# Hybrid decoder step: weight sums with two rooms and a step of lag, raw blocks loaded from ScalarE's queue, phase turn and gate-weight loads rearranged

## What is computed

```
h  = rms_norm(x) * (1 + scale(c)) + shift(c)
layer 0: q,k,v,z,gate = h @ w_in_ab       # GLA and RetNet, chunked linear attention
         y = (norm(attention) * silu(z)) @ w_out_ab
layer 1: qkv, z, b, a = h @ w_in_c        # gated DeltaNet; qkv through a causal convolution of width 4
         y = (norm(delta) * silu(z)) @ w_out_c
x  = x + gate(c) * rms_norm(y)
```

## Time and profile before

| | |
|---|---|
| median of 3 runs | 2617.94 us (2615.05 to 2620.39) |
| the profiled execution, its own time | 2615.59 us |
| its span in the profile | 2613.8 us |
| TensorE busy | 2371.3 us (91%) |
| VectorE, ScalarE, GpSimd busy | 1416.1, 968.0, 872.4 us |
| mean granted clock of TensorE, of full speed | 0.957 |
| phases by the first and last TensorE instruction | inab to 722, mixab 728 to 1118, inc 1125 to 1782, mixc from 1793 us |

### The profile page before, as it was taken

How to read it: one execution, slowest core, us unless ns; L and a number is a source line. 1 busy time by engine, 2 the same in 40 slices (tenths; PEclk the granted TensorE clock), 3 DMA queues, 4 the chain that set the end, 5 groups by cost and what they waited for, 6 DMA issues and landing times. The chain is left out here.

```text
span 2613.8 us, 58705 instructions
## 1 busy us (share of the span) xinstructions
PE 2371.3 (91%) x23067; PEld 1693.5 (65%) x23084; DVE 1416.1 (54%) x3034; ACT 968.0 (37%) x2726; POOL 872.4 (33%) x1092
## 2 busy tenths in 40 slices
PE   6989679679979999769999999996999999999997
PEld 2434234234555655258888888785888888888885
DVE  3332544534057785547777585555646555564655
ACT  3533244233311111324444343433444454444431
POOL 2541122121111111112322122115655656565652
PEclk9999899889989999879999999998999999999997
DMA  8543575572346444586676667556523222222213
GB/s 296 149 143 102 154 213 144 165 217 77 113 133 234 154 160 148 167 276 213 213 213 215 198 198 228 179 165 184 133 65 94 79 83 91 83 91 75 82 38 85
DMA packets 371527, 395.26 MB, mean 151 GB/s; under 512 B 39215, under 2 KB 262511, under 8 KB 371298
## 3 DMA queue, kind: packets, MB, share of 16 engines
q1 hardware_dynamic: 337186, 360.28, 43.8%
q10 hardware_dynamic: 34112, 31.71, 4.0%
HBM read 275.19 MB, written 116.72 MB: 150 GB/s over the span
## 5 line engine op out<-in xcount | busy, mean ns | idle before, releaser
L2728 DVE SCALAR_TENSOR_TENSOR inc_acc<-inc_ub,inc_taps,inc_acc 128x512 f32<-128x512 f32 x288 | 243.7, 846 | 9.2 <-ACT inc_acc L2571 2.4
L742 PE MATMUL inab_b<-inab_wt,keep 128*128 128x512 f16 x768 | 172.6, 387 | 30.9 <-ACT inab_vz L1064 20.0
L742 PE MATMUL inab_b<-inab_wt,raw_next 128*128 128x512 f16 x768 | 173.8, 390 | 21.1 <-ACT inab_vz L1064 21.1
L2507 POOL COPY inc_halo<-inc_ub 128x3 f32<-128x3 f32 x96 | 50.2, 525 | 363.6 <-DVE inc_ub L2716 224.1
L1344 PE MATMUL mixab_y<-keep,mixab_oT_hi 128*128 128x512 f16 x512 | 152.4, 379 | 7.1 <-DVE mixab_f_y L1424 5.4
L742 PEld LDWEIGHTS inab_b<-inab_wt,keep 128*128 128x128 bf16 (+1 forms) x768 | 75.9, 99 | 125.7 <-ACT inab_vz L1064 22.2
L742 PEld LDWEIGHTS inab_b<-inab_wt,raw_next 128*128 128x128 bf16 (+1 forms) x768 | 76.5, 100 | 117.3 <-ACT inab_vz L1064 23.3
L726 POOL TENSOR_TENSOR inab_a_out<-inab_stage,inab_a_out 128x384 f16<-128x384 f32 x64 | 61.3, 958 | 226.9 <-ACT inab_a_out L719 226.9
L712 DVE TENSOR_TENSOR inab_stage<-inab_m,inab_stage 128x512 f16<-128x512 f32 x64 | 44.1, 689 | 135.9 <-ACT inab_stage L722 135.9
L2837 PE MATMUL inc_b<-inc_room,keep 128*128 128x256 bf16 (+3 forms) x864 | 109.9, 279 | 2.4 <-DVE stage_next L2698 2.4
L3201 POOL TENSOR_TENSOR mixc_levels<-mixc_BT,raw_next 128x512 f32<-128x512 f32 (+1 forms) x82 | 110.3, 1376 | 1.5 <-DVE mixc_BT L3487 1.5
(11 more groups left out here) (619 smaller groups left out, 6363.4 us busy)
## 6 DMA issues: line engine op xcount, KB each, us to landing
keep<-tmp_w SPq DMA_DIRECT2D x336, 256.0 KB, 3.2
tmp_qkv<-inc_acc SPq DMA_DIRECT2D x96, 256.0 KB, 2.6
inab_stage<-in_w_in_c SPq DMA_DIRECT2D x128, 128.0 KB, 2.5
...
tmp_w<-inab_a_out SPq DMA_DIRECT2D x64, 192.0 KB, 2.1
...
```

The source lines that it names most:

```text
L742: last = nc.tensor.matmul(dst, lhs(a, k), rhs(b, k), start=(k == 0 and i == 0), stop=(k == KT - 1 and i == len(PASSES) - 1))
L2507: pool.tensor_copy(halo[:, g, :], ub[w % 2][side][:, BLK:]).then_inc(halo_saved[side], 1)
L2728: ins = dve.scalar_tensor_tensor(a_v, u_[:, i:i + BLK], taps[:, g, i:i + 1], a_v, ALU.mult, ALU.add)
```

## The change

- **The pair weights.** `a_out` gets two rooms. On ScalarE the high halves of the sums of step n are made in step n + 1 (`sums_hi`), on VectorE the low halves of the sums two steps later, and SyncE's store of them is issued two steps later. The raw quarters of step n + 1 are loaded from ScalarE's queue in step n, no longer from SyncE's.
- **Which groups.** No step lies at g = 10, 15 and 16 any more, and three groups instead of seven have two. Blocks 1 and 2 have 25 steps each, block 3 has 14. The eight steps of the output weights move to g = 23 to 30 of block 3.
- **SyncE's order.** The store of `r` and the loads of x tiles move to later places among the stores of v and z, and the waits for `u` and `r` to have landed move to g = 24. Two small tables are loaded late, into the room of `a_out`.
- **The turn.** `scale_high` and the copy of `eye2` come before the last state update, GpSimd's part of the halves is dropped; VectorE makes three of the seven low parts, partly between the last steps of mixab, and the four that are left at the start of inc (`first_left`). The second ring slot is loaded at the start of inc instead of the end of mixab.
- **inc.** The z weights are loaded in eight smaller transfers at units 1, 2, 5 and 8. `ORDER` has five qkv units first, and the last two units of a block are z. The last tail rows and sample convolution move to unit 15 of the last block, before the last unit's final products.

```diff
+        if n >= 2:
+            self.store_s(sp, n - 2)
         sp.wait_ge(self.a_lo, n + 1)
-        sp.dma_start(self.dst[u, 0:3, :, k].rearrange("m p e x -> p m e x"), self.a_out[:]).then_inc(self.a_stored, 16)
-        if n + 2 < PAIR_STEPS:
-            sp.wait_ge(self.s_done, n + 1)
-            self.load(sp, n + 2)
-        if n >= 1:
-            self.store_s(sp, n - 1)
+        sp.dma_start(self.dst[u, 0:3, :, k].rearrange("m p e x -> p m e x"), self.a_out[n % 2]).then_inc(self.a_stored[n % 2], 16)
...
+        if n >= 2:
+            self.sums_lo(dve, n - 2)
         dve.wait_ge(self.raw_in[n % 2], 32 * (n // 2 + 1))
-        wait(dve, self.s_hi, n - 1)
         wait(dve, self.s_lo, n - 1)
...
     def hi(self, act, n):
 
+        if n >= 1:
+            self.sums_hi(act, n - 1)
+            if n + 1 < PAIR_STEPS:
+                act.wait_ge(self.a_lo, n)
+                self.load(act, n + 1)
         act.wait_ge(self.raw_in[n % 2], 32 * (n // 2 + 1))
-        wait(act, self.a_stored, 16 * n)
-        act.activation(self.a_out[:, :, 0, :], self.raw[n % 2][:, P:4 * P].rearrange("p (m x) -> p m x", m=3), ACT.Copy).then_inc(self.a_hi, 1)
+        wait(act, self.a_stored[n % 2], 16 * (n // 2))
+        act.activation(self.a_out[n % 2][:, :, 0, :], self.raw[n % 2][:, P:4 * P].rearrange("p (m x) -> p m x", m=3), ACT.Copy).then_inc(self.a_hi, 1)
+
+    def sums_hi(self, act, n):
         act.wait_ge(self.s_done, n + 1)
         wait(act, self.s_stored[n % 2], 16 * (n // 2))
         act.activation(self.s_out[n % 2][:, :, 0, :], self.banks[n % 2][:].rearrange("p (m x) -> p m x", m=4), ACT.Copy).then_inc(self.s_hi, 1)
...
-    W7_TWICE = (16, 18, 20, 22, 24, 26, 28)
-    w7_slots = [g for g in order(BLK) for _ in range(2 if g in W7_TWICE else 1) if not 5 <= g < 7]
-    W7_BLOCK = len(w7_slots)
+    W7_SLOTS = (0, 1, 2, 3, 4, 7, 8, 9, *range(17, 31))
+    W7_TWICE = (20, 24, 28)
+    w7_slots = [g for g in W7_SLOTS for _ in range(2 if g in W7_TWICE else 1)]
...
     def w7_at(b, g):
 
-        return [(b - 1) * W7_BLOCK + i for i, s in enumerate(w7_slots) if s == g] if 1 <= b <= 2 else []
-
-    assert 2 * W7_BLOCK == PAIR_STEPS
+        if b == nb - 1:
+            first = (nb - 2) * W7_BLOCK
+            return [first + i for i, s in enumerate(W7_SLOTS) if s == g and s < W7_LAST]
+        return [(b - 1) * W7_BLOCK + i for i, s in enumerate(w7_slots) if s == g] if 1 <= b < nb else []
+
+    ROWS_AT = {W7_LAST + i: i for i in range(KT)}
+    assert (nb - 2) * W7_BLOCK + sum(s < W7_LAST for s in W7_SLOTS) == PAIR_STEPS
...
+            w7_next(b, 0, 1)
+            next_x(0)
+            w7_next(b, 2, 3, 4, 7, 8)
+            next_x(1)
+            w7_next(b, 9)
+            store_u()
...
                 w7_next(b, 15 + j)
-                if j == 4:
...
+                if j == 1:
+                    next_x(2)
+                if j == 3:
+                    store_r()
+                if j == 6:
                     next_x(3)
+                if j == 9:
+                    sp.wait_ge(out, 80 * (b + 1))
+                    sp.sem_inc(u_free, 1)
+                    sp.sem_inc(r_free, 1)
...
+                  [stage_next[:, i * D:(i + 1) * D].rearrange("p (k n) -> p k n", k=4) for i in (2, 3, 0, 1)])
+    io["first_left"] = early.left()
...
-        for u in range(2):
-            for m in FIRST_NEEDED:
-                sp.dma_start(ring_slot(io, u)[:, m].rearrange("p k e x -> p (k e x)"), io["w7"][u, m].rearrange("p k e x -> p (k e x)")
-                             ).then_inc(io["ring_in"][u][m], 16)
+        first_weights(sp, io, 0)
...
-        early.lower_rest(pool)
...
+        early.upper_sums(act, (0, 1, 2))
         fin.square_sample(act, nt)
+        early.upper_sums(act, (3,))
...
         for p in range(PAIRS):
+            if p == PAIRS - 1:
+                early.scale_high(dve)
+                dve.tensor_copy(eye2.rearrange("p (e c) -> p e c", e=2), bc(tv["eye_h"].unsqueeze(1), [P, 2, HB])).then_inc(eye_ready, 1)
...
-        early.scale_high(dve)
         dve.wait_ge(cond.mm, 6)
...
-        early.lower(dve)
-        dve.wait_ge(o_done, nt + 1)
-        dve.tensor_copy(eye2.rearrange("p (e c) -> p e c", e=2), bc(tv["eye_h"].unsqueeze(1), [P, 2, HB])).then_inc(eye_ready, 1)
+        early.lower_first(dve)
         fin.mean_sample(dve, nt)
+        early.lower(dve, 2)
         dve.wait_ge(gate_in, 48)
         fin.gated_sample(dve, nt, 0, 16 * (nt // 2 + 2))
+        early.lower(dve, 1)
...
-    ORDER = (0, 1, 2, (0, 0), 3, 4, 5, (0, 1), 6, 7, 8, (1, 0), 9, 10, 11, (1, 1))
+    ORDER = (0, 1, 2, 3, 4, (0, 0), 5, 6, (0, 1), 7, 8, 9, 10, 11, (1, 0), (1, 1))
...
+        tiles.load(sp, 0)
+        sp.dma_start(wab_raw, io["w_in_c"].rearrange("(k p) n -> p k n", p=P)[:, :, N_C - 32:N_C]).then_inc(wab_in, 16)
+        first_weights(sp, io, 1)
+        tiles.load(sp, 1)
         load_tables(sp, tab_in, tab, names, io["table"])
...
-        for v in range(4):
-            sp.dma_start(zw[:, v].rearrange("p m k e x -> p m (k e x)"), io["w7"][QKV + v].rearrange("m p k e x -> p m (k e x)")
-                         ).then_inc(zw_in[v // 2], 16)
-        sp.dma_start(alog[:, 0, :], io["a_log_c"].unsqueeze(0).to_broadcast([P, H])).then_inc(small_in, 16)
-        sp.dma_start(alog[:, 1, :], io["dt_bias_c"].unsqueeze(0).to_broadcast([P, H])).then_inc(small_in, 16)
...
+        def load_zw(v):
+            for ms in (slice(0, 4), slice(4, 7)):
+                sp.dma_start(zw[:, v, ms].rearrange("p m k e x -> p m (k e x)"), io["w7"][QKV + v, ms].rearrange("m p k e x -> p m (k e x)")
+                             ).then_inc(zw_in[v // 2], 16)
+
+        ZW_AT = {1: 0, 2: 1, 5: 2, 8: 3}
...
+                if n in ZW_AT:
+                    load_zw(ZW_AT[n])
...
+                if p == 15:
+                    sample_silu(2)
+                    take_tails(2)
...
+        for dst, src, hi in io["first_left"]:
+            dve.tensor_tensor(dst, src, hi, ALU.subtract).then_inc(first_lo, 1)
...
+                if p == 15:
+                    sample_conv(2)
...
+            if n == 0 and i in FIRST_LEFT:
+                pe.wait_ge(first_lo, FIRST_LEFT[i])
```

More of the change, by code:

```diff
@@ L661, in __init__ @@
         self.src, self.dst, self.raw, self.s_out, self.banks = src, dst, raw, s_out, banks
-        self.a_out = ph.sb("a_out", [P, 3, 2, P], F16)
+        self.room = ph.sb("a_out", [P, 6 * P])
+        self.a_out = [self.room[:, i * 3 * P:(i + 1) * 3 * P].bitcast(F16).rearrange("p (m e x) -> p m e x", m=3, e=2) for i in range(2)]
         s = ph.sem
@@ L968, in _ @@
         sp.wait_ge(pre_in, 64)
-        sp.wait_ge(w7.a_stored, 16 * PAIR_STEPS)
-        for i in range(2):
-            sp.wait_ge(w7.s_stored[i], 16 * PAIR_STEPS // 2)
+        w7.stored(sp, w7.s_stored)
         for i in range(4):
@@ L1006, in _ @@
                     w7.lo(pool, step)
-        prep.rstd(pool, nt, 0, NS)
-        prep.split_lo(pool, nt, 0, NS, prep.at(nb))
-        for u in range(KT):
-            rows_out.lo(pool, u)
+        for g in order(BLK):
+            if g == SQUARE[0]:
+                prep.rstd(pool, nt, 0, NS)
+            if g == HI_S:
+                prep.split_lo(pool, nt, 0, NS, prep.at(nb))
+            for step in w7_at(nb - 1, g):
+                w7.lo(pool, step)
+            if g in ROWS_AT:
+                rows_out.lo(pool, ROWS_AT[g])
     @block.scalar
@@ L1099, in groups @@
                 if g in rows_at:
+                    if g == W7_LAST:
+                        w7.sums_hi(act, PAIR_STEPS - 1)
+                        w7.raw_free(act)
+                        rows_out.load(act, 0)
+                        w7.stored(act, w7.s_stored)
                     rows_out.hi(act, rows_at[g])
@@ L1108, in _ @@
             groups(b, BLK, [(4 * b + 4 + tc, P) for tc in range(4)])
-        w7.room_free(act)
-        rows_out.load(act, 0)
-        groups(nb - 1, BLK, [(nt, NS)], rows_at={**dict(zip(range(16, 30, 2), range(7))), 30: 7})
+        groups(nb - 1, BLK, [(nt, NS)], rows_at=ROWS_AT)
         groups(nb, NS, [])
@@ L1139, in w7_sums @@
                 for step in w7_at(b, g):
[L1140 to L1141 removed]
                     w7.sums(dve, step)
+                if b == nb - 1 and g == W7_LAST:
+                    w7.sums_lo(dve, PAIR_STEPS - 2)
+                    w7.sums_lo(dve, PAIR_STEPS - 1)
         def work(b, n, next_tiles):
```

129 lines of the change are left out of this document (69 added, 60 removed).

## The result

The changed kernel takes 2475.49 us in the median of four runs (2470.28 to 2478.14), beside 2616.49 of the kernel before, measured along with it. The ratio is 0.9458, with a 95% interval of 0.9435 to 0.9482.

What follows compares the result with a forecast made beforehand. TensorE was taken to set the pace, with idle and low-clock time to give back. From 2615.59 us, -96 - 10 - 8.5 + 1.5 - 3 = -116 gave 2499.6, stated as 2501 allowing for scatter; range 2488 to 2530.

Steps and rivals of the forecast that it cites:

- read the stretches from block start to block start: First reading step, on inab: blocks 1 and 2 take 177.73 and 181.83 us, block 3 134.66; 38 and 42 us idle.
- Blocks 1 to 3: -96: inab, pair weights: blocks fall to 132, 132 and 130 us, together -96 us (bounds -84 and -106).
- 4 us that I leave for waits that this reading misses: Blocks 1 to 3 of inab: 4 us taken off the 100.3 us gain, leaving -96.
- The second room takes the 4.1 us loop off ScalarE: Pair weights in inab: ScalarE's step becomes about 3.6 us with waits, against 5.22 us of a TensorE group.
- the groups 10, 15 and 16, during which VectorE rotates `r`, carry no step: inab: with SyncE's later wait for `r`, said to change the row of ScalarE's 18.04 us wait; no separate size.
- Rival B: inab blocks: half of the block stalls stay, gain 50 instead of 96 us, about 2547 us; chance 0.14.
- D: inab blocks: ScalarE, with the issues on its queue, becomes the bound and the kernel is slower, 2664 us; chance 0.03.
- The turn: -10: Between mixab and inc: difference no longer stretched, reduction not waiting for the copy; -10 us (bounds -6 and -12).
- inc: -7: inc: start -8.5 us from spreading the z transfers (bounds -9.5 and +8), body +1.5 us.
- The +1.5 for `sample_conv`: Body of inc: of its 4.7 us of VectorE work in the last unit, 1.4 don't fit; +1.5 us (0 to 4).
- Rival C: Units 1 to 3 of inc: z transfers delay ring refills, the 8.5 us return as a wait, 2517 us; chance 0.10.
- The end: -3: Step from inc to mixc: only the last unit's own eviction and store are left; -3 us (0 to -5).

Runs made afterwards that it cites:

- r_first: Changed kernel, but SyncE stores r and waits for u and r to have landed ahead of a block's first store of v; 2496.8 us, ratio 0.954.
- before_r_late: Kernel before, but SyncE stores r behind the fourth store of v, x tiles 2 and 3 load later, u and r waits at g = 24; 2585.6 us.
- spread: Changed kernel with 25, 25 and 14 steps but none doubled, so g = 10, 15 and 16 carry a step each in blocks 1 and 2; 2473.8 us.
- old_groups: Changed kernel with the steps at the groups of before: 32 each in blocks 1 and 2, seven groups doubled, none in block 3; 2519.4 us.
- only_groups: Changed kernel with one room for a_out, no lag of the sums, and r stored and landed ahead of the first v store; 2512.0 us.
- avoid: Changed kernel with 32, 32 and 0 steps in blocks 1 to 3, g = 10, 15 and 16 free, ten groups doubled; 2518.8 us.
- gpsimd_low: Changed kernel, but GpSimd makes one of the seven low parts at the end of mixab, beside VectorE's differences; 2480.3 us, ratio 0.948.

## Why the prediction was wrong, point by point

**Block 0 isn't in the sum: 11.1 us.** The step that failed is the first one, "read the stretches from block start to block start", in which I took blocks 1 to 3 for all that could give something back. The order of SyncE's stores is the same in block 0. Its length of 154.7 us, 20 more than block 3 of the same trace, and ScalarE's 15.05 us wait were there to be read. r_first put 9.8 us of it back, before_r_late took 10.1 out. It is the largest part of the miss, not all of it. The spans fell by 142.6 us where the sum has 116: the 26.6 between them are 11.1 here, 7.7 in blocks 1 to 3, 0.2, 3.5 and 1.9 in the turn, inc and its end, 5.0 in mixc, less 2.8 by which head and mixab grew. With block 0 in the sum the forecast is 2490 and the range 2477 to 2519, and 2475.5 still lies 1.4 us below it.

**Blocks 1 to 3: -96 against -103.7.** The lengths were forecast at 132, 132 and 130 and came at 131.05, 131.04 and 128.39, 3.5 us in all; the other 4.2 are the "4 us that I leave for waits that this reading misses". There were none. That the lengths came near owes something to how they were made: 132 is TensorE's own work with nearly every wait taken away, so it holds whichever edit takes them away.

**The reasons given for that term were right only in part.** "The second room takes the 4.1 us loop off ScalarE" is worth 14 to 15 us, not the bulk of 104. That "the groups 10, 15 and 16, during which VectorE rotates `r`, carry no step" is worth nothing (spread). What the sum gave no part to, 25 steps instead of 32 in a block with three doubled groups instead of seven, is the largest part (43 us in old_groups, up to 77 in only_groups). My own numbers half pointed there: I had 3.6 us for a single step's group and 6.3 to 7.5 for a doubled one against 5.22. At the upper end a pair of them takes 11.1 us where TensorE takes 10.44, which isn't given back when every second group is doubled, and is when only every fourth is. I applied this to the changed kernel only, not to the one before.

**Rival B** (half of the stalls stay) and D (ScalarE sets the pace) didn't come. B is what old_groups and avoid show: with 32 steps TensorE stays idle for 12 to 18 us in each of blocks 1 and 2 (38 and 42 before).

**The turn: -10 against -10.2.** Both steps held: the difference at 1.23 us and the reduction no longer behind the copy. gpsimd_low brings the stretched difference back with GpSimd's part (3.04 us), and as in the kernel before it ends 1.1 us behind GpSimd's end.

**inc: -7 against -10.5.** The first 19 products, units 0 to 2 but for the last two of unit 2, took 41.7 us with the small products for the gates before and 32.2 now, -9.5, which is the bound I gave and cut to 8.5. TensorE's one wait inside unit 0 grew from 0.28 to 0.68 us, so the four low parts left for the start cost no more than 0.4. The +1.5 for `sample_conv` didn't come: the rest of the phase is 1.0 us shorter. Rival C, a collision of the z transfers at units 1 and 2, isn't there. Whether the new ORDER has part in the 1.0 wasn't tried.

**The end: -3 against -4.9.** The last unit's store is all that is left, SyncE's last issue comes 1 to 2 us behind TensorE's last product instead of 7. This was read in the two traces and not tried by itself.

**mixc: 0 against -5.0.** No edit touches it. In the eleven other profiles with the same mixc it took 816.4 to 823.7 us, and 819.1 in before_r_late; the time at the lower clock differs between them too (35 to 56 us), though not in step with the lengths. So I take the 5.0 as scatter, not gain.
